# A two-block transformer kernel on one core: the entry to the second block by halves of the tokens, three of its tiles begun early, and reciprocals of the head norms in quarters

## What is computed

```
y = (o * silu(z)) @ mla_w_out          # last product of the first block, 2048 -> 1024
h = h + rmsnorm(y, post_norm[1])       # drop the meta tokens: x, 512 tokens
# second block, with a context of 256 tokens
pc = project(modulate(ctx, norm1_g, csh1, csc1), w_in)   # rmsnorm(.)*(1+scale)+shift, then @ w_in
px = project(modulate(x,   norm1_g, sh1,  sc1),  w_in)
down = gate columns of px, pc;  log_alpha = log_sigmoid(down @ gate_up + bias) / 16
# gated linear attention needs cumulative sums of log_alpha
# differential attention, 4 heads of 4 query blocks; each head's output is normalised:
od = rmsnorm(od, diff_norm_g) * 0.8
```

## Time and profile before

| | |
|---|---|
| median of 3 runs | 2238.53 us (2238.3 to 2239.27) |
| the profiled execution's own time | 2238.49 us |
| its span | 2236.70 us |
| mean granted clock of PE | 0.989 of full speed |
| PE busy | 2150.1 us |
| DVE busy | 971.3 us |
| ACT busy | 715.0 us |

### The profile page before, as it was taken

How to read it: one execution, slowest core, us unless ns; L and a number is a source line. 1 busy time by engine, 2 the same in 40 slices (tenths; PEclk the granted TensorE clock), 3 DMA queues, 4 the chain that set the end, 5 groups by cost and what they waited for, 6 DMA issues and landing times.

```text
span 2236.7 us, 37225 instructions
## 1 busy us (share of the span) xinstructions
PE 2150.1 (96%) x16267; PEld 1577.1 (71%) x16267; DVE 971.3 (43%) x1885; ACT 715.0 (32%) x1369; POOL 0.2 (0%) x4
## 2 busy tenths in 40 slices
PE   6999999999999988999999997999998999999999
PEld 5788888788888875555555543575575578888888
DVE  2655555555553113233323103553356555466522
ACT  4434344334332113444444214433544430000000
POOL 0000000000000000000000000000000000000000
PEclk9999999999999999999999998999999999999999
DMA  5313222222131321111111212211000215323230
GB/s 178 96 57 96 77 65 88 77 66 88 58 95 58 114 71 33 33 33 58 41 52 38 76 38 66 72 40 58 19 1 1 76 38 146 94 78 92 71 122 19
DMA packets 200603, 150.06 MB, mean 67 GB/s; under 512 B 16360, under 2 KB 198122, under 8 KB 200058
## 3 DMA queue, kind: packets, MB, share of 16 engines
q1 hardware_dynamic: 200442, 147.69, 22.3%
HBM read 143.41 MB, written 4.26 MB: 66 GB/s over the span
## 4 chain that ended last, share of the span: by engine, by line
PE 91%; DVE 5%; ACT 2%; issue 1%; DMA 0%; SPq 0%; DVEq 0%; ACTq 0%
PE PS L2403 15%; PE PS L1616 12%; PE PS L1626 6%; PE PS L713 5%; PE PS L775 5%; PE PS L451 4%; PE PS L1368 4%; PE PS L1377 3%; PE PS L1370 3%; PE PS L719 2%; PE PS L1547 2%; PE PS L836 2%; PE PS L756 2%; PE PS L757 2%; PE PS L2531 1%; PE PS L2519 1%
## 5 line engine op out<-in xcount | busy, mean ns | idle before, releaser
L2403 PE MATMUL PS<-hn_all,ring 128*128 128x264 f32 x1536 | 397.0, 393 | 0.0
L2403 PEld LDWEIGHTS PS<-hn_all,ring 128*128 128x128 f32 x1536 | 276.4, 190 | 45.3 <-issue 3.7
L713 PE MATMUL PS<-hn_all,ring 128*128 128x512 f32 x256 | 115.0, 592 | 0.0
L775 PE MATMUL PS<-big,ring 128*128 128x512 f32 x256 | 111.2, 592 | 0.0
L451 PE MATMUL PS<-big,ring 128*128 128x264 f32 x416 | 92.7, 386 | 0.0
L1368 PE MATMUL PS<-ring,hn_all 128*128 128x256 f32 x384 | 88.9, 385 | 2.5 <-ACT scr L1824 2.5
L775 PEld LDWEIGHTS PS<-big,ring 128*128 128x128 f32 x256 | 48.2, 190 | 58.3 <-issue 57.7
L451 PEld LDWEIGHTS PS<-big,ring 128*128 128x128 f32 x416 | 79.0, 190 | 13.5
L914 ACT ACTIVATE scr<-PS,scr 128x528 f32<-128x528 f32 (+1 forms) x64 | 34.6, 541 | 165.8 <-DVE scr L1001 165.6
L1616 PE MATMUL PS<-scr 128*128 128x256 f32 x352 | 84.0, 380 | 1.8 <-DVE scr L2144 1.7
L1616 PE MATMUL PS<-hn_all,scr 128*128 128x256 f32 x352 | 83.3, 379 | 0.4 <-DVE hn_all L2152 0.4
(11 more groups left out here) (475 smaller groups left out, 3810.5 us busy)
## 6 DMA issues: line engine op xcount, KB each, us to landing
ring<-in_w_mod SPq DMA_DIRECT2D x24, 1024.0 KB, 5.4
ring<-in_gdn_w_in SPq DMA_DIRECT2D x16, 1024.0 KB, 5.5
ring<-in_w_in SPq DMA_DIRECT2D x12, 1024.0 KB, 5.5
hn_all<-in_w_ffn_in SPq DMA_DIRECT2D x22, 512.0 KB, 5.2
ring<-in_w_ffn_in SPq DMA_DIRECT2D x22, 512.0 KB, 5.3
ring<-in_mla_w_in SPq DMA_DIRECT2D x9, 1024.0 KB, 5.4
ring<-in_gdn_w_in SPq DMA_DIRECT2D x16, 512.0 KB, 5.1
ring<-in_gdn_w_out SPq DMA_DIRECT2D x8, 1024.0 KB, 6.7
```

Of the source, the lines that this page charges most:

```text
L713: ins = mm(o, wz_pair(p)[:, k, j * P:(j + 1) * P], hq[:, k, :], start=(k == 0), stop=(k == KD - 1))
L775: ins = mm(PS[:, MOUT[m % 2], :], wslot(m % 4, P, 16)[:, k, :], oq[:, k, :], start=(k == 0), stop=(k == 15))
L2403: ins = mm(o, wslot(slot_, 256)[:, k, m * P:(m + 1) * P], hn[:, k, b * HALF:(b + 1) * HALF], start=(k == 0), stop=(k == KD - 1))
```

## The change

The work is computed as before, up to the order of sums. What differs:

- Row tiles 4 to 7 of y are made in halves of 256 tokens, first half of all four, then second half (`M_UNITS`, twelve units j in all). `yq` and `mtmp` lie elsewhere in `scr`.
- The means are taken from sums that DVE forms, not by eight matmuls: the context's by one matmul inside unit 6 (`sqs_d` 1), the first half's post-norm mean by one inside unit 8, its second-block mean by one inside unit 10; the second half's post-norm mean by two matmuls after the first two of tile 0's, its second-block mean by three.
- Scaling, residual, squares, Ln and Exp, products and shifts are done for the context, the first half and the second half in turn, on ACT and DVE between the y evictions. Three table loads are asked for by hand.
- PE begins tiles 0, 1 and 2 on the first 512 columns of `xm` (context and first half, in `in_rows(n, 0, ...)`) and finishes them in `ORDER`'s places on the last 256.
- SP loads each `w_in` slot once the second-half unit that used its ring slot is done; the gate weights and tables are asked for ahead of them, from the context's transposes on.
- The reciprocal of `merge_c` is done as four of 128x128 (`merge_r`), spread over three units; for the last head all four stand together.

```
+        M_UNITS = [(m_, slice(0, SEQ)) for m_ in range(4)] + [(m_, x_) for x_ in TOKEN_HALVES for m_ in range(4, KD)]
...
-            for m in range(2, KD):
+            for j in range(2, len(M_UNITS)):
+                m, x = M_UNITS[j]
                 pe.wait_ge(*up("mo%d" % (m % 4), 16 * (m // 4 + 1)))
-                pe.wait_ge(*up("mo_sq", m - 1))
-                out_rows(m, range(16))
+                pe.wait_ge(*up("mo_sq", j - 1))
+                out_rows(j, range(8))
+                if j == 6:
+                    pe.wait_ge(*up("sqs_d", 1))
+                    mm(PS[:, 6, 0:CTX], const("mean_d"), sq2[:, 0, 0:CTX], start=True, stop=True).then_inc(s["ms2"], 1)
+                if j == 8:
+                    pe.wait_ge(*up("mo_acc", 8))
+                    mm(PS[:, 3, 0:SEQ // 2], const("mean_d"), gacc[:, 0:SEQ // 2], start=True, stop=True).then_inc(s["mo_ms"], 1)
+                if j == 10:
+                    pe.wait_ge(*up("sqs_d", 2))
+                    mm(PS[:, 6, CTX:SEQ], const("mean_d"), sq2[:, 0, CTX:SEQ], start=True, stop=True).then_inc(s["ms2"], 1)
+                out_rows(j, range(8, 16))
...
-                if m == 6:
-                    pe.wait_ge(*up("sq2_d", 1))
-                    for k in range(KD):
-                        ins = mm(PS[:, 2, 0:CTX], const("mean_d"), sq2[:, k, 0:CTX], start=(k == 0), stop=(k == KD - 1))
-                    ins.then_inc(s["ms2"], 1)
-            pe.wait_ge(*up("mo_acc", KD))
-            mm(PS[:, 4, 0:SEQ], const("mean_d"), gacc[:, 0:SEQ], start=True, stop=True).then_inc(s["mo_ms"], 1)
...
+            evict(4)
+            evict(5)
+            in_scale(0)
+            shifted(0)
+            evict(6)
+            nc.scalar.preload_act_table_set("natural_log")
+            evict(7)
+            out_scale(0)
+            evict(8)
+            squares(0)
+            evict(9)
+            in_scale(1)
+            evict(10)
+            shifted(1)
+            nc.scalar.preload_act_table_set("natural_log")
+            evict(11)
+            out_scale(1)
+            nc.scalar.preload_act_table_set("natural_log")
+            squares(1)
+            in_scale(2)
+            shifted(2)
...
+            def squares_sum(n):
+                x = XM_PARTS[n]
+                dve.wait_ge(*up("sq2_d", (1, 9)[n]))
+                for k in (4, 2):
+                    link(V.tensor_tensor(sq2[:, 0:k, x], sq2[:, 0:k, x], sq2[:, k:2 * k, x], ALU.add))
+                V.tensor_tensor(sq2[:, 0, x], sq2[:, 0, x], sq2[:, 1, x], ALU.add).then_inc(s["sqs_d"], 1)
...
+            for k in range(KD):
+                if k < KD - 1:
+                    out_scaled(k + 1)
+                residual(k)
+            squared(8)
+            squares_sum(1)
+            squared(9)
+            in_scaled(1)
+            squared(10)
+            dve.wait_ge(*up("mo_rstd", 2))
+            dve.wait_ge(*up("mout_ev", len(M_UNITS)))
+            out_scaled(KD)
+            x = XM_PARTS[2]
+            for k in range(KD):
+                if k < KD - 1:
+                    out_scaled(KD + k + 1)
+                residual(KD + k)
+                if 2 <= k:
+                    dve.wait_ge(*up("sq2_d", KD + k + 1))
+                    if k > 2:
+                        dve.wait_ge(*up("sqs_d", k))
+                    if k < 7:
+                        V.tensor_tensor(sq2[:, 0, x], sq2[:, 0, x], sq2[:, k - 1, x], ALU.add).then_inc(s["sqs_d"], 1)
+            in_scaled(2)
...
         def b2_sp(sp):
-            sp.wait_ge(*up("mout", KD))
-            sp.wait_ge(*up("mres", KD))
...
-            sp.wait_ge(*up("xm_d", 16))
+            sp.wait_ge(*up("cx_tr", NCTX))
             sp.dma_start(T2, t["tables2"][:, MASK_W:TAB2_W]).then_inc(s["tab2_in"], 16)
             sp.dma_start(masks, t["tables2"][:, 0:MASK_W]).then_inc(s["tab2_in"], 16)
+            for n in range(4):
+                sp.wait_ge(*up("mout", 9 + n))
+                in_slot(n)
...
+            pe.wait_ge(*up("ii0", 16))
+            in_rows(0, 0, 0, 2)
+            pe.wait_ge(*up("mo_acc", 11))
+            pe.wait_ge(*up("mo_sq", 12))
+            mm(PS[:, 3, SEQ // 2:SEQ], const("mean_d"), gacc[:, SEQ // 2:SEQ], start=True, stop=False)
+            mm(PS[:, 3, SEQ // 2:SEQ], const("mean_d"), gsqb[1][:, SEQ // 2:SEQ], start=False, stop=True)\
+                .then_inc(s["mo_ms"], 1)
+            in_rows(0, 0, 2, KD)
+            pe.wait_ge(*up("ii1", 16))
+            in_rows(1, 0, 0, KD)
+            in_rows(2, 0, 0, 2)
+            pe.wait_ge(*up("sqs_d", 7))
+            for k in (0, 6, 7):
+                if k:
+                    pe.wait_ge(*up("sq2_d", KD + k + 2))
+                ins = mm(PS[:, 6, 0:CTX], const("mean_d"), sq2[:, k, SEQ:TOK2], start=(k == 0), stop=(k == 7))
             ins.then_inc(s["ms2"], 1)
+            in_rows(2, 0, 2, KD)
...
+            if u_ % 4 == 3 and 4 < u_ < 15:
+                ORDER += [("merge_r", u_ // 4 - 1, 1)]
+            if u_ % 4 == 0 and u_ > 4:
+                ORDER += [("merge_r", u_ // 4 - 2, 3), ("merge_c", u_ // 4 - 2)]
             if u_ < 15:
                 ORDER += [("soft", u_ + 1)]
             if u_ % 4 == 2 and u_ > 4:
-                ORDER += [("merge_c", u_ // 4 - 1)]
+                ORDER += [("merge_r", u_ // 4 - 1, 0)]
+            if u_ % 4 == 3 and u_ > 4:
+                ORDER += [("merge_r", u_ // 4 - 1, k_) for k_ in ((2,) if u_ < 15 else (1, 2, 3))]
+            if u_ == 15:
+                ORDER += [("merge_c", 2)]
...
+            def merge_r(h, part):
+                x = slice(part * P, (part + 1) * P)
+                dve.wait_ge(*up("osr", h + 1))
+                link(V.reciprocal(osq[:, x], osq[:, x]))
+
             def merge_c(h):
                 om = mix[:, 4 + h, :]
-                dve.wait_ge(*up("osr", h + 1))
                 dve.wait_ge(*up("oss_d", h + 1))
-                link(V.reciprocal(osq, osq))
```

More of the change, by code:

```diff
@@ L489, in gemm_out_act @@
                     continue
[L490 to L506, removed]
+                act.wait_ge(*up("gout", m + 1))
+                nc.scalar.activation(two(y[:, m, :]), halves(b), ACT.Copy).then_inc(s["gout_ev"], 1)
@@ new lines, in gemm_out_act, with gemm_out_dve @@
+                act.wait_ge(*up("go_acc", m - 1))
+                nc.scalar.activation(two(gsqb[m % 2]), halves(b), ACT.Square).then_inc(s["go_sq"], 1)
+            act.wait_ge(*up("go_ms", 1))
+            act_link(nc.scalar.activation(two(grs), halves(6), ACT.Ln, bias=eps))
+            nc.scalar.activation(grs, grs, ACT.Exp, scale=-0.5).then_inc(s["go_rstd"], 1)
+        def gemm_out_dve(dve, gain, y, h):
+            for m in range(2):
+                dve.wait_ge(*up("gout", m + 1))
+                nc.vector.tensor_tensor(two(y[:, m, :]), halves(2 * m), two(acc[m]), ALU.add).then_inc(s["gsum"], 1)
@@ L963, in mla_act, with evict @@
-            gemm_out_act(act, "m", yq, lambda ap: ap[:, 0:SEQ], lambda b: PS[:, {0: MOUT[0], 2: MOUT[1], 4: 4}[b], :], context)
+            def evict(j):
+                m, x = M_UNITS[j]
+                o = PS[:, MOUT[j % 2], x]
+                act.wait_ge(*up("mout", j + 1))
+                A(yq[:, m, x], o, ACT.Copy).then_inc(s["mout_ev"], 1)
+                if j >= 2:
+                    act.wait_ge(*up("mo_acc", j - 1))
+                A(gsqb[j % 2][:, x], o, ACT.Square).then_inc(s["mo_sq"], 1)
@@ new lines, in mla_act @@
+            for j in range(4):
+                evict(j)
+            for n in range(NCTX):
+                act.wait_ge(*up("cx_tr", n + 1))
+                ins = A(ctxT[:, :, n * P:(n + 1) * P],
+                        PS[:, CTX_BANK[n]:CTX_BANK[n] + 2, :].rearrange("p b (k n) -> p (b k) n", n=P), ACT.Copy)
+            link(ins)
+            A(sq2[:, :, 0:CTX], ctxT, ACT.Square).then_inc(s["sq2_d"], 1)
+            evict(4)
+            evict(5)
+            in_scale(0)
+            shifted(0)
@@ L1228, in two_blocks @@
                 ORDER += [("gate_silu",)]
-        ORDER += [("gated",), ("mixed", 0), ("merge_a", 3), ("merge_b", 3), ("merge_c", 3), ("mixed", 1), ("mixed", 2), ("mixed", 3)]
+        ORDER += [("gated",), ("mixed", 0), ("merge_a", 3), ("merge_b", 3)] + [("merge_r", 3, k_) for k_ in range(4)]
+        ORDER += [("merge_c", 3), ("mixed", 1), ("mixed", 2), ("mixed", 3)]
         MBANK = (0, 1, 4, 5)
@@ L2915, in _ @@
             out_rstd(QK_HEADS - 1)
-            gemm_out_act(act, "g", yT, two, halves)
+            gemm_out_act(act, yT)
             mla_act(act)
```

192 lines of the change are left out of this document (117 added, 75 removed).

## The result

The changed kernel takes 2212.2 us (median of 4 runs, 2211.24 to 2214.77) against 2238.7 beside it: a ratio of 0.9883 (0.987 to 0.9895), thus 26.5 us gained. I had forecast 2215.0, a gain of 23.5, with a range of 2208 to 2224. The profiled execution has a span of 2210.6 us, 26.1 less than before.

What follows compares the result with a forecast made beforehand. PE, busy 96% of the span, was taken to bound the kernel by its work plus its holes. 2238.5 less 17.4 up to `diag` and 6.1 for the reciprocals gave 2215.0 us, range 2208 to 2224.

Steps and rivals of the forecast that it cites:

- Units by halves: y tiles at second-block entry: eight units of 32 instructions take 55.3 us, ending at 1362.8, with evictions costing nothing.
- rival (d): First half's DVE and ACT chain ends behind unit 10, PE waits, half of 17.4 goes: 2223.6 us; 4%.
- Rival (e): Weight loads no longer hide behind 256-column matmuls: fully exposed 48.6 us more, 2263.5 us; 3%.
- The second half's chain covered: Second-block entry: 48 instructions of tiles 0 to 2 cover the DVE and ACT chain, leaving no PE hole.
- Two instructions of 512 columns, 0.430 each, for `down`: Tile 0's `down` matmuls priced as whole ones: first part 6.9 us, last part 3.5.
- rival (a): `down` matmuls overlap about 2.4 at a time, tile 0's first part falls to 2.9 us: 2211.9 us; 12%.
- The gate's serial chain of 17.4 us to the second copy: DVE and ACT gate work, 16.6 us plus a 0.8 copy, leaves PE holes of 1.1 and 2.7 before tiles 3 and 4.
- The lower clock after them: Tile 4, behind the hole: 1.0 us added for a lower clock, ends 0 and 2.5.
- DVE and the level steps: After `diag`: DVE's idle 5.49 us is used up, level steps stay bound by PE, 0 to 2 us lost.
- Rival (b): Gate chain costs more: lower clock through tiles 3 and 4, level steps bound by DVE, 2219.5 us; 15%.
- Reciprocals: Head merges: quarters of 0.98 us shorten PE's waits before `turn` in heads 0 and 1; 6.1 us gained.
- The charge of 0.5 for PE's idling ahead of `mixed(0)`: Head 2: no gain, PE idles more on the way, 0.5 us charged; ends 2 lost, 1 gained.

Runs made afterwards that it cites:

- uneven strips: Changed kernel with `down` matmuls put unevenly on four strips (k = 0, 1, 2 on their own, 3 to 7 on the fourth): 2213.96 us.
- the copies first: Changed kernel with ACT's copies of tiles 1 and 2 moved ahead of the two `sig_a` in the written order: 2210.01 us.
- the third copy moved as well: Kernel with both moves, and ACT's copy of tile 4 also moved ahead of `kd_a`: 2206.99 us.
- quarters alone: Kernel before the change with the reciprocals in quarters and nothing else: 2234.8 us against 2239.68.
- both moves: Changed kernel with copies of tiles 1 and 2 ahead of `sig_a`, and head 2's last quarter and `merge_c` behind the gate product: 2204.31 us, again 2204.8.
- the gate product first: Changed kernel with head 2's last reciprocal quarter and `merge_c` moved behind the gate product on DVE: 2208.77 us.
- the cover behind: Changed kernel with the begun parts of tiles 0 to 2 placed behind the second half's two means: 2220.6 us.

## Why the prediction was right, and where its terms were off

The range held and the sign was right; 2212.2 lies 2.8 us under the forecast. That it came so near is in part luck: 6.7 us of gain that I had not forecast stand against 4.1 of loss that I had not forecast either (the sum at the end of this section). Term by term, with the same bounds as in the working:

- **Units by halves: right.** Forecast 55.3 us for eight units, measured 1307.16 to 1363.71 less three means of 0.43, 55.3. No PE idle, so the queues of ACT and DVE held, and rival (d) falls. Their end was forecast at 1362.8 and came at 1363.71; of the difference, 0.94 had come in ahead of the change. Rival (e) falls with it: 0.216 us an instruction with a weight load for each.
- **The second half's chain covered: right.** The last square ends at 1376.1, forecast 1376.5 to 1378.5; PE asks for the sum at 1376.38 and doesn't wait. PE was 2.7 us ahead of its forecast there (1379.1), and DVE and ACT just far enough ahead of theirs: 0.28 us are left between the last square and the mean.
- **"Two instructions of 512 columns, 0.430 each, for `down`" is the step that failed**, and the term that was mis-sized: I laid the 16 instructions of tile 0's first part in at 6.9 us and its last part at 3.5. They take about 3.0 (0.98 for four and 2.0 for twelve) and 1.9, the latter set by ACT's shifts and not by the strips. That is rival (a), which I gave 12%. The gate products begin at 1386.46 and, less the 0.94, at 1385.5, 5.3 earlier than the 1390.8 of the working (1393.4 less the gate product's 2.6). The uneven strips show the mechanism. The Trainium skill, TensorE: Matmul & The Clock Gate, Part 3, has column strips run side by side with 2.38x for three. The trace agrees that they do; here four strips take 16 instructions in about 3.0 us instead of 6.9, 2.3x.
- **I had said rival (a) would keep 1 us less, waiting for the squares. That wait didn't come** (no idle at L1519), and the rival left tile 0's last part at 3.5, so even it was priced short.
- **The gate's serial chain of 17.4 us to the second copy: right.** From DVE's first gate operation (1390.01) to the end of tile 2's copy (1407.35) pass 17.34. The holes at tiles 3 and 4, forecast 1.1 and 2.7, are 1.21 and 2.37. The kernel with the copies first, which has neither, shows that this order is what made them.
- **The lower clock after them: mis-sized.** I put 1.0 on tile 4; it cost 1.9 (8.81 over 6.9, granted clock 0.81), within the bound of 2.5. `diag` came 111.65 us after the transposes, forecast 115.93 by the working (1420.4 less 1304.47): 4.3 better.
- **DVE and the level steps:** I had left ends of 0 and 2 lost. They gained 1.6. In the kernel before, a hole of 1.43 us with no releaser stood at 1443.12; it isn't in the new trace. Rival (b) is half right: the holes cost tile 4 more than I took, but the level steps stayed with PE. (The first one waits for DVE only with the third copy moved as well, 2.15 us.)
- **Reciprocals, 6.1 forecast, 5.4 to 6.4 measured** (6.4 between the medians on one chip, 6.4 and 5.4 by legs). The parts: a quarter 0.94 for 0.98. Head 0 gained 3.45 for 3.0, head 1 3.67 for 3.65. The slack of about 1 us at u = 8 and 12 held: `turn` doesn't wait there. Head 2 up to `mixed(0)` gained 0.1 for 0. The charge of 0.5 for PE's idling ahead of `mixed(0)` was 2.1, just past my own bound of 2.
- **Not forecast at all:** 1.55 us at 1659.89, where eight instructions run slowly behind an idle of 2.46 at ACT. It goes neither with the new entry nor with the quarters. These eight and the eight behind them take 5.05 to 5.11 us together in twelve of the fourteen traces, quarters alone among them, and 3.47 in two: the kernel before, and one of the two profiles of the kernel with both moves. So this term of the ledger is what the same code does one time and not another, and it can't be put down to the change.

The sum by the two traces: 23.5 forecast, plus 4.3 at `diag`, 1.6 behind it, 0.2 at the level steps and 0.55 at the heads; less 1.55 at 1659.89, 1.6 at `mixed(0)` and 0.94 ahead of the change: 26.1.

## What to carry to other kernels

Where a serial chain on slow engines stands between two stretches of matmuls, halving the tokens costs the tensor engine nothing as long as 256 columns run at half the time of 512 (here 0.216 and 0.430 us), and the work begun early should be cut to just outlast the chain. Then look at once for which queue now holds the buffers: here ACT's copy behind a Ln was the next wait, and moving it ahead in the written order brought `diag` 4.4 us forward, of which a lower clock and a hole behind it took more than half back. Price small column strips by the fullest strip and by the engine that feeds them, not by the number of instructions. Compare profiles by legs from a point ahead of the change, and before a slow stretch is put down to a change, look whether a kernel with the same code up to there has it too.

## What the runs showed of the hardware that I had not expected

- **Strips run side by side out of order.** Neighbours in the same strip (pairs) cost nothing over a run of 32 instructions, 10.64 us to 10.62. In the trace the twelve of the kernel with pairs start in threes, one from each strip, 0.013 us apart and 0.43 to 0.45 us from three to three, though in the written order the four of one strip stand together. Within a strip they are serial: 1.83 for four.
- **The same hole doesn't always cost the same.** Tile 4 stands 2.37 us for ACT in eight traces. It then takes 8.8 us at a granted clock of 0.81 in both traces of the changed kernel, with pairs, with uneven strips and with the gate product first, and 7.12 at 1.00 in both traces with whole reciprocals and with the cover behind, by PE's part of the chain:

```profile
1404.67 7.12 PE PS L1537 x16
```

  Here each kernel that was profiled twice repeats itself. The eight instructions behind ACT's table load don't: behind an idle of 2.46, the kernel with both moves takes 1.97 us for them in one profile and 2.55 in the other, and the eight behind them 1.50 and 2.55. What decides it is not settled by these runs.
- **A hole without a releaser.** In the kernels with the copies first, PE stands 0.5 to 1.1 us in the tile behind the first level step, for nothing the profile shows, as it did ahead of it in the kernel before (1.43) and with quarters alone (1.31). In the second run of the kernel with both moves:

```profile
1425.23 1.49 PE PS L1546 x4
1426.71 0.53 issue
```

  In all six traces with such a hole a packet of the queue that brings in instructions starts 1.0 to 1.9 us ahead of it (here at 1424.83). In the changed kernel such packets come too, at 1420.94 and 1425.73, and PE has no hole. So that they are the cause is argued and not shown.
